# A mixer and grouped-expert layer on one Trainium2 core: the first expert's rows gathered whole and turned by TensorE, and copies, splits, gathers, scatters and norms in another order

## The reference

```python
def hybrid_mixer(x, w_in, b_in, conv_w, mh_g, w_out):
    p = x @ w_in + b_in
    ...
    return jnp.concatenate([y_m, y_c], axis=-1) @ w_out

def grouped_moe(x, router_w, router_b, w_gate, w_up, w_down):
    probs = jax.nn.softmax((xf @ router_w).astype(jnp.float32) + router_b.astype(jnp.float32), axis=-1)
    ...
    def expert_block(args):
        xb, e = args
        hdn = jax.nn.silu(xb @ w_gate[e]) * (xb @ w_up[e])
        return hdn @ w_down[e]
    ...
    y = y_buf[dest] * gate_sorted[:, None].astype(x.dtype)
    return jnp.zeros_like(xf).at[tok_sorted].add(y).reshape(b, s, d)

def reference(...):
    for l in range(DEPTH):
        mix = hybrid_mixer(x, w_in[l], b_in[l], conv_w[l], mh_norm_g[l], w_out[l])
        x = layer_norm(ALPHA * x + mix, ln_mix_g[l], ln_mix_b[l])
        ffn = grouped_moe(x, router_w, router_b, w_gate[l], w_up[l], w_down[l])
        x = layer_norm(ALPHA * x + ffn, ln_moe_g[l], ln_moe_b[l])
    return x
```

## Time and profile before

| | us |
|---|---|
| median of 3 runs | 1645.46 |
| lowest and highest | 1643.64 and 1649.17 |
| the profiled execution's own time | 1650.94 |
| its span, first to last instruction | 1649.4 |
| PE busy in the span | 1558.1 (94%) |
| DVE, ACT, POOL busy | 1125.3, 664.6, 478.2 |

### The profile page before, as it was taken

One profiled execution on the slowest core, in us unless ns is written; L12 is line 12 of the kernel. 1 busy time (PEld: TensorE's weight loads), 2 busy tenths in 40 slices (PEclk: granted clock), 3 DMA queues, 4 the chain that ended last, 5 costly groups with the idle time before them and its releaser, 6 DMA issues. The chain is left out here.

```text
span 1649.4 us, 24119 instructions
## 1 busy us (share of the span) xinstructions
PE 1558.1 (94%) x9044; PEld 1345.6 (82%) x9044; DVE 1125.3 (68%) x1859; ACT 664.6 (40%) x908; POOL 478.2 (29%) x378
## 2 busy tenths in 40 slices
PE   8999999999999999999999819999999999999993
PEld 6888887888878888878888619899988989899883
DVE  4536867657857658586568666676777768677876
ACT  3224424144333243342243334444555445445552
POOL 2100017100045000072000043444445555445543
PEclk9999999999999999999999959999999999999997
DMA  7422335322426222534224444776778697858782
GB/s 245 145 86 77 126 130 184 124 77 96 161 94 213 77 77 102 177 130 154 77 77 138 159 159 160 228 221 217 246 242 257 215 265 235 263 207 251 256 256 96
DMA packets 120885, 276.24 MB, mean 167 GB/s; under 512 B 17169, under 2 KB 19345, under 8 KB 120257
## 3 DMA queue, kind: packets, MB, share of 16 engines
q1 hardware_dynamic: 92544, 187.63, 33.7%
q0 software_dynamic: 27648, 84.96, 17.5%
q10 hardware_dynamic: 576, 2.10, 0.3%
HBM read 229.66 MB, written 48.40 MB: 169 GB/s over the span
## 5 line engine op out<-in xcount | busy, mean ns | idle before, releaser
L1308 PE MATMUL mix_acc<-kept_xT,mix_w_high 128*128 128x512 f32 x640 | 256.5, 401 | 6.1 <-DVE mix_w_low L961 3.2
L1707 POOL DMA_INDIRECT moe_x_quarter_rows<-x,kept_places x144 | 173.9, 1208 | 288.9 <-DVE moe_xT_low L2003 181.5
L1310 PE MATMUL mix_acc<-kept_xT,mix_w_low 128*128 128x512 f32 x640 | 250.9, 392 | 0.0
L1309 PE MATMUL mix_acc<-kept_xT,mix_w_high 128*128 128x512 f32 x640 | 250.1, 391 | 0.0
L961 DVE TENSOR_TENSOR mix_w_low<-mix_w_raw,mix_w_high 128x2048 fp32r<-128x2048 f32 x71 | 170.8, 2406 | 105.9 <-ACT mix_w_high L769 105.6
L769 ACT ACTIVATE mix_w_high<-mix_w_raw 128x2048 fp32r<-128x2048 f32 x71 | 136.0, 1915 | 233.7 <-PE mix_acc L1310 233.7
L1969 DVE TENSOR_TENSOR moe_gate_up_low<-kept_w_gate_up_raw,moe_gate_up_high 128x2048 fp32r<-128x2048 f32 x64 | 146.5, 2289 | 91.6 <-ACT moe_gate_up_high L1825 73.8
L2355 PE MATMUL moe_gate_psum<-moe_xT_high,moe_gate_up_high 128*128 128x288 f32 x512 | 153.7, 300 | 26.0 <-issue 21.5
L2356 PE MATMUL moe_gate_psum<-moe_xT_low,moe_gate_up_high 128*128 128x288 f32 x512 | 151.5, 296 | 1.6 <-issue 1.6
L2355 PE MATMUL moe_up_psum<-moe_xT_high,moe_gate_up_high 128*128 128x288 f32 x512 | 151.6, 296 | 1.4 <-issue 1.4
L2356 PE MATMUL moe_up_psum<-moe_xT_low,moe_gate_up_high 128*128 128x288 f32 x512 | 151.4, 296 | 1.4 <-issue 1.3
(11 more groups left out here) (475 smaller groups left out, 3457.4 us busy)
## 6 DMA issues: line engine op xcount, KB each, us to landing
mix_w_raw<-in_w_in SPq DMA_DIRECT2D x56, 1024.0 KB, 5.3
kept_w_gate_up_raw<-in_w_gate SPq DMA_DIRECT2D x32, 1024.0 KB
kept_w_gate_up_raw<-in_w_up SPq DMA_DIRECT2D x32, 1024.0 KB
queries_keys_or_down_raw<-in_w_down SPq DMA_DIRECT2D x32, 1024.0 KB
mix_w_raw<-in_w_out SPq DMA_DIRECT2D x16, 1024.0 KB, 5.0
kept_conv_or_residual<-in_x POOLq DMA_DIRECT2D x16, 512.0 KB, 5.3
mix_x_rows<-in_x POOLq DMA_DIRECT2D x12, 512.0 KB, 4.5
x<-mix_x_rows POOLq DMA_DIRECT2D x12, 512.0 KB, 3.5
```

What stands on the lines that cost most here:

```text
L1308: pe.matmul(out, ah, bh, start=first, stop=False)
L1309: pe.matmul(out, ah, bl, start=False, stop=False)
L1310: return pe.matmul(out, al, bh, start=False, stop=last)
L1707: pool.indirect_dma_start(out=X[:, m], out_offset=None, in_=x_quarters, in_offset=bass.IndirectOffsetOnAxis(ap=gather_i[:, at:at + 1], axi ...
```

## The change

1. Expert 0's tiles A and B are gathered as whole rows, one indirect DMA of 128 x 4 KB each (`gather_first`), by row numbers that DVE writes before PE's spread matmul (`first_rows`, semaphore `first_ready`). PE turns them with 32 fp32 matmuls against the identity for each tile, four column tiles side by side, into PSUM (`turn_first`); ACT and DVE split them from there (`first_high`, `first_low`). U of expert 0 is gathered as before, after `gather_ready`. ORDER becomes (A, B, U).
2. The mixer's quarter copy of x1 and its DMA go from POOL to ACT (`store_x1`), in stages 1 and 2 of the next group, after `turned_rows`. POOL's multiplication by alpha waits for it.
3. The y copies of A and B are all on ACT (`y_rows`, two of 128x512 for each tile); DVE's `y_half` is gone.
4. In each expert the splits of weights n+4 and n+5 stand at the end, n+2 at the start, and n+3 right after the first sigmoid (ACT) or first hidden product (DVE). `row_norm(e - 1, 1)` goes behind the split of n+4, `row_stats` before that of n+5.
5. On POOL, gathers and scatters are interleaved: gather A, scatter A, gather B, gather U, scatter B, scatter U, then list_store.

```diff
-    ORDER = (U, A, B)
+    ORDER = (A, B, U)
...
+            def gather_first(r, k):
+                m = BLOCKS[k]
+                pool.indirect_dma_start(out=X[:, m[0]:m[-1] + 1].rearrange("p m n -> p (m n)"), out_offset=None,
+                                        in_=x1_dram,
+                                        in_offset=bass.IndirectOffsetOnAxis(ap=first_rows[:, k:k + 1], axis=0))\
+                    .then_inc(x_in[k], 16)
...
+            def first_high(r, k):
+                act.wait_ge(turned[k], r * NE + 1)
+                for part, bank in enumerate(first_at[k]):
+                    c = slice(4 * part, 4 * part + 4)
+                    ins = act.activation(xTh[:, c, AT[k]], bank[:].rearrange("p (c n) -> p c n", c=4), ACT.Copy)
+                ins.then_inc(xh_done, 1)
...
+            def first_low(r, k):
+                dve.wait_ge(xh_done, low_rows(r, 0, k)[1])
+                for part, bank in enumerate(first_at[k]):
+                    sl = (slice(None), slice(4 * part, 4 * part + 4), AT[k])
+                    ins = dve.tensor_tensor(xTl[sl], bank[:].rearrange("p (c n) -> p c n", c=4),
+                                            xTh[sl].bitcast(F32), ALU.subtract)
+                ins.then_inc(xl_done, 1)
...
+            def turn_first(r, k):
+                wait_apart(pe, idle, *landed(r, 0, k))
+                m = BLOCKS[k]
+                for c in range(KC):
+                    for j in range(QUARTERS):
+                        ins = pe.matmul(first_at[k][c // 4][j * UT:(j + 1) * UT, c % 4 * P:(c % 4 + 1) * P],
+                                        X[:, m[j], c * UT:(c + 1) * UT], keep.ident[:], start=True, stop=True)
+                ins.then_inc(turned[k], 1)
...
+            def store_x1(n, t):
+                act.wait_ge(v.x1_ready, n * NT + t + 1)
+                act.wait_ge(xt_ps, n * NT + 2 * NT)
+                if t >= 2:
+                    act.wait_ge(x1_out[t % 2], n * (NT // 2 * 16) + 16)
+                act.activation(by_quarters(XN[:, t % 2]), by_chunks(R[:, t]), ACT.Copy).then_inc(quarters, 1)
+                act.wait_ge(quarters, n * NT + t + 1)
+                act.dma_start(x1_dram[bass.ds(n * GT + t * P, P)], XN[:, t % 2]).then_inc(x1_out[t % 2], 16)
...
+                own.step(dve.tensor_scalar(tok[:, 0, 0:2], psl[:, 0:2], -1.0, 0.0, ALU.add, ALU.max))
+                own.wait(r)
+                dve.tensor_copy(first_rows, tok[:, 0, 0:2]).then_inc(first_ready, 1)
...
                 for e in range(NE):
                     n = e * FC
-                    split_gu(r, n + 1)
+                    if e == 0:
+                        split_gu(r, 1)
+                    split_gu(r, n + 2)
                     hidden(r, e, 0)
-                    split_gu(r, n + 2)
+                    split_gu(r, n + 3)
                     h_low(r, e, 0)
                     row_norm(r, e - 1, 0, 1)
-                    split_gu(r, n + 3)
...
-                    row_norm(r, e - 1, 1)
                     for k in ORDER:
                         x_low(r, e + 1, k)
-                    y_half(r, e, A)
                     split_gu(r, n + FC)
+                    row_norm(r, e - 1, 1)
                     if e != LAST:
                         row_stats(r, e)
-                    y_half(r, e, B)
+                    split_gu(r, n + FC + 1)
```

More of the change, by code:

```diff
@@ L1770, in _ @@
             with pool.Fori(0, wanted) as r:
+                wait_apart(pool, idle, first_ready, r + 1)
+                for k in (A, B):
+                    gather_first(r, k)
                 wait_apart(pool, idle, gather_ready, r + 1)
-                for k in ORDER:
-                    gather(r, 0, k)
+                gather(r, 0, U)
                 for k in ORDER:
@@ L1777, in _ @@
                 for e in range(LAST):
-                    for k in ORDER:
-                        gather_next(r, e + 1, k)
+                    gather_next(r, e + 1, A)
+                    scatter(r, e, A)
+                    gather_next(r, e + 1, B)
+                    gather_next(r, e + 1, U)
+                    scatter(r, e, B)
+                    scatter(r, e, U)
                     if e:
                         list_store(r, e - 1)
-                    for k in range(COLS):
-                        scatter(r, e, k)
                     if e + 1 in BATCH:
@@ L1860, in y_half @@
                     act.wait_ge(added, r * (LAST * COLS * 16) + e * (COLS * 16))
-                act.activation(Y[:, k, 0:BANK], (py, pb)[k][0][:], ACT.Copy,
-                               scale=gate[:, COLS * e + k:COLS * e + k + 1]).then_inc(y_act, 1)
+                for q in range(2):
+                    ins = act.activation(Y[:, k, q * BANK:(q + 1) * BANK], (py, pb)[k][q][:], ACT.Copy,
+                                         scale=gate[:, COLS * e + k:COLS * e + k + 1])
+                ins.then_inc(y_done, 1)
             def y_quarters(r, e):
@@ L1924, in _ @@
                     split_gu(r, n)
-                for k in ORDER:
-                    x_high(r, 0, k)
+                for k in (A, B):
+                    first_high(r, k)
+                x_high(r, 0, U)
                 act.wait_ge(scatter_ready, r + 1)
```

78 lines of the change are left out of this document (34 added, 44 removed).

## The result

The changed kernel takes 1622.68 us (median of 4 runs, 1621.62 to 1624.59), the kernel before 1647.32 beside it (4 runs, 1643.64 to 1650.25): ratio 0.9848, 95% interval 0.9813 to 0.9882. That is 24.6 us less. I had forecast 10.7 less and a range that ends at 1626.0, so the direction was right and the size less than half of what came.

A forecast was written before the change was run, and what follows sets the result against it. PE was taken as the bound, busy 1558.1 of 1649.4 us. Join -3.8 and borders -6.9 sum to -10.7 us, from the median 1645.46 to 1634.8 us; range 1626 to 1643.2.

The forecast's parts named there:

- Join: Where mixer meets experts: whole-row gathers and PE's turn start the first gate/up matmul at 981.0 instead of 984.82, -3.8 us.
- only the borders: Rival, chance 0.07: the tiled turn is slow, 6.3 us per tile, PE starts 2.7 us later; 1641.3 us.
- warm rival: Rival, chance 0.16: both gains, expert 0 at full clock (-2.1), five other PE waits without a releaser gone (3.0); 1629.7 us.
- better bound of the join: At the join of mixer and experts: everything at full clock and the fast landing, -5.8 us.
- slow-turn rival: At the join: records set the turn's time, B's turn ends at 983.3, PE starts at 987.5; chance 0.07.
- Order of the splits: Borders between experts: SP issues the next weights 5 us earlier, 11.1 us into the expert; the border waits go, -6.9 us.
- six borders: Of 15 borders between experts, the six longer than 1.87 us; windows sum to 18.11 us, 6.9 us of it waits.
- first part: What bounds the kernel: PE, with 91 idle us and its slow clock to win; join and late borders named as waits.
- GpSimd's order: Gathers and scatters in the experts: B's and U's gathers slip by one scatter, 3.2 us at most; priced at 0.
- y copies: ACT at the borders: +0.69 us ahead of the next split, 1.2 us of slack; priced at 0.
- x1 copy: Mixer: copies move from POOL to ACT, the low part for stage 3 still 2 us ahead; priced at 0.
- slower rival: Rival, chance 0.10: ACT becomes the bound at the border, each us over 1.2 costs 15 us; 1654.3 us if 2.5 late.

## Why the prediction was wrong in its size

- **Join.** Right, step by step. Gathers at 966.50, 967.84 and 969.10 (forecast 966.7, 968.0, 969.3), A's turn from 970.93, 3.64 us long (970.7, 3.7), B's end about 976.3 (976.6), PE at 980.18 (981.0): 4.6 us where I had 3.8, 4.9 in the run without it. The turn runs at the speed of plain fp32 matmuls, 64 records in 3.64 us at half clock; the rule that column tiling shuts transpose mode off for fp32, in the Trainium skill's "TensorEngine Tiling (Array Packing)", Restrictions, agrees with that speed. The rival "only the borders" (records count, 6.3 us per tile) is out. That the clock would rise during the turn also held: 64 records in 3.64 us, then 32 in 1.13. Gate/up began at full clock (980.18) and fell to half 1.0 us later, up to 984.4 (0.94 in the mean of that stretch), so the warm rival's 2.1 us came only as 0.5. The landing took at most 970.93 - 966.50 = 4.4 us, and PE started when the DMA released it. I had used 3.9. The estimate of 3.2 us, worked out from the Trainium skill's "DMA: Bandwidth & Descriptors", Anatomy of one DMA, is further from that 4.4. Two of the recorded sums were slips: the better bound of the join, full clock and fast landing, comes to 7.0 us by its own terms and not 5.8, which would have put the low end of the range at 1624.7, still above what came; and in the slow-turn rival PE starts at 987.7, not 987.5.
- **Order of the splits, as to borders.** Right: SP issues the weights 11.2 us into every expert but 0 (forecast 11.1; expert 14 starts at 1518.97, its load at 1530.17), and the six borders went, 6.9 us. The 16.3 us that I took for today's issue is that of one expert: over the experts it was 13.8 to 22.5, and ahead of two of the six late borders only 13.8, so that the issue moved up by 2.6 us there and not by 5. The landing followed: with the issue early, the DMA engines fall to a share of 0.22 and 0.42 before the border at 1442.5, where the last border of the kernel before had 1.08:

```profile
1431.20:1434.20 3.00, 3.00 (x15) 2.46 (x14) 2.49 (x4) 1.70 (x3) 0.01 (x1) 1.00 0.95 358
1434.20:1437.20 3.00, 3.00 (x15) 2.49 (x14) 0.59 (x2) 1.83 (x3) 2.39 (x3) 1.00 0.22 66
1437.20:1440.20 3.00, 3.00 (x15) 2.49 (x14) 1.73 (x1) 3.00 (x2) 2.39 (x3) 1.00 0.42 115
```

- **The step that failed** stands at the end of the first part: "The rest of the idle time is at the start, in the router's tail and in short pauses in the experts; the change doesn't touch it." The only reason given, under the warm rival, was the releaser "issue"; what the gate/up splits waited for stands in no sentence of it. The pauses lengthened the experts by 16 us, some 8 of them among the traced 91 idle ones and the rest in PE's busy time (expert 11's half clock above all). They were waits for the split of n+1 behind y_quarters, and in expert 6 for that of n+2 behind a sigmoid. I had ACT's 28.3 us "remote" for y_quarters within reach in the table of waits (its seven times are ahead of experts 2, 3, 4, 5, 9, 10 and 11, all of which pause), and that the new order takes the split of n+1 out from behind it is in the diff. I priced what the new order does for n+4 only. The warm rival named the right kind of wait, "the five other waits without a releaser", but not the right price. Of its 3.0 us 2.1 are two waits at the first matmul of experts 9 and 11 (0.9 and 1.2 us), late borders that the 6.9 us had already counted. Most of the pauses' idle time stands in five other rows of the same table, 6.1 us in 15 waits, all inside gate/up stretches:

```profile
PE moe_gate_psum L2356 <- issue: 1.6, 4, 0.8
...
PE moe_up_psum L2357 <- issue: 1.4, 3, 0.9
PE moe_up_psum L2355 <- issue: 1.4, 3, 0.7
PE moe_up_psum L2356 <- issue: 1.3, 3, 0.7
...
PE moe_gate_psum L2357 <- issue: 0.4, 2, 0.2
```

  The other half of their cost is in PE's busy time, where no row of the waits can show it. A stretch's length against the floor of 25.26 would have shown all of it.
- **GpSimd's order** was priced at 0 and is worth 0 where both the new splits and the y copies on ACT are there, but 9.7 us without the new splits (1641.9 against 1632.3). In the kernel before, alone, it brings the ratio to 0.986. Parts that cover for one another can't be added: splits alone 0.990, GpSimd's order alone 0.986, join 4.9 us, and all together 0.985 to 0.989 in two sets.
- **y copies, x1 copy, tile order.** The first two are worth nothing each in the changed kernel, as priced; the tile order wasn't undone there, and in the kernel before it is worth nothing. Together with GpSimd's order they were worth 5.6 us beside the new splits (1633.2 against 1627.6), which prices of 0 for each one could not show. The slower rival (ACT the bound at the border) didn't come: in the changed kernel all 15 borders are on the floor.

Not settled is what holds PE's last-rows signal back by 1.5 to 7 us. It goes with gathers issued over the border and with DVE's half of the y copies; in the kernel before, moving either brings it back on time at nearly all borders. But neither alone is the cause throughout: with the y copies on ACT, the old splits and GpSimd's old order y_quarters was late again by 0.7 to 3.3 us at most borders. What it is, or whether the transfers behind them matter, no run here shows.

## What to carry to other kernels

Price idle time by stretch, as length minus the length of an undisturbed one, and not by the table of waits: a wait for operands may be spread over the matmuls ahead of it under the name "issue". For each instruction that a new order moves, look at what stood behind it in its queue as well as at what it feeds. Where a raw buffer is refilled once per round, count the cycle (issue, landing, split, first use) against PE's own time for the round: while that cycle is the longer one, much of a pause that is taken away elsewhere comes back at the border (here 15 us of borders with only y_quarters moved), and an earlier issue ended it here. And a part that is worth nothing when it alone is taken out may still be worth something together with another.

## What the runs showed of the hardware

- A kernel's scatter can go with its slack. With the cycle near its limit the kernel with GpSimd's order alone took 1631 to 1649 us within five runs, and the kernel before had medians of 1638, 1647, 1652 and 1657 in different sets (not all on one chip); the changed kernel, whose splits are always in time, stayed within 1620.7 to 1624.6 in two sets. It isn't a rule: old splits with halved y copies had four late borders and stayed within 1631.3 to 1632.4. The gain is 16 us beside the quickest before and 25 beside the one first measured.
- A semaphore of PE may be seen by two other engines at the same moment several us after the matmul that carries it has its record (1.6 us in four experts, 7.1 in one), while PE goes on.
- How long PE idles doesn't alone tell whether half clock follows. In the changed kernel it did after 3.9 us at the join, though the first 1.0 us of matmuls still ran at full clock. With tile U first PE idled 2.60 us in both traces, and half clock followed in one (26.55 us for expert 0's gate/up) and not in the other (25.25). At the first late border of the kernel with the new splits alone it followed after 2.43 us, expert 7's gate/up taking 26.8 us.
